# A mixer rebuilt: sums moved into the projections, branch b scaled between remainders, a norm's halves overlapped

## What is computed

```python
xn = rmsnorm(x)
h_a, c_a, b_a, v_b, g_b = split(xn @ w_in)                 # five groups of 512 channels
y_a = rmsnorm(b_a * dwconv(c_a * h_a, 3 taps))             # branch a
y_b = rmsnorm(silu(layernorm(dwconv(v_b * sigmoid(g_b), 31 taps) + bias)))   # branch b
h = x + concat(y_a, y_b) @ w_out
out = rmsnorm(h + peer(rmsnorm(h)))   # 8 heads, top 16 of 128 x 128 single-neuron experts each
```

## Time and profile before

| what | value |
|---|---|
| median of 3 runs | 1464.48 us (1464.34 to 1467.53) |
| profiled execution | 1464.40 us, span of its instructions 1462.6 us |
| PE busy | 1446.8 us, 99% |
| VectorE, ScalarE, POOL busy | 1232.1, 627.1, 880.1 us |
| mean granted clock of TensorE | 0.996 |

### The profile page before, as it was taken

The page is one execution under the profiler, slowest core; times in us unless marked ns, Lnnn a source line. Parts: engine busy times, 40 slices in busy tenths (PEclk is TensorE's granted clock), DMA queues, the critical chain, the costliest instruction groups (busy, mean ns, idle before and its releaser), DMA issues.

```text
span 1462.6 us, 25025 instructions
## 1 busy us (share of the span) xinstructions
PE 1446.8 (99%) x8592; PEld 1322.5 (90%) x8592; DVE 1232.1 (84%) x2517; ACT 627.1 (43%) x845; POOL 880.1 (60%) x551
## 2 busy tenths in 40 slices
PE   9998989999999999999999999999999999999998
PEld 9998989999999999999999999888888888888886
DVE  6998876899999999588788841799999999999995
ACT  6335543333333333566666654333333333333333
POOL 5687534556888888767666765255555555555510
PEclk9999999999999999999999999999999999999999
DMA  5321223567999999779999999899999999999962
GB/s 195 101 86 58 91 73 119 199 217 241 314 343 346 345 346 341 259 291 381 359 367 359 376 361 374 327 370 386 388 399 376 405 378 398 374 407 379 382 250 90
DMA packets 120260, 433.35 MB, mean 296 GB/s; under 512 B 12385, under 2 KB 12641, under 8 KB 118529
## 3 DMA queue, kind: packets, MB, share of 16 engines
q1 hardware_dynamic: 62592, 212.88, 40.5%
q0 software_dynamic: 46080, 167.79, 30.3%
q10 hardware_dynamic: 11520, 51.93, 8.9%
HBM read 379.34 MB, written 52.69 MB: 295 GB/s over the span
## 4 chain that ended last, share of the span: by engine, by line
PE 85%; DVE 0%; issue 0%; DVEq 0%; ACT 0%
PE ps_unit L861 37%; PE ps_misc L930 25%; PE ps_unit L930 12%; PE ps_unit L834 6%; PE ps_misc L896 3%; PE ps_misc L799 1%; PE ps_misc L803 0%; PE ps_unit L786 0%; PE ps_misc L926 0%; PE ps_unit L926 0%; PE ps_misc L915 0%; PE ps_misc L817 0%; DVE rows L1480 0%; DVE ps_unit L1478 0%; DVE hot_i L1649 0%
## 5 line engine op out<-in xcount | busy, mean ns | idle before, releaser
L515 POOL TENSOR_TENSOR w_lo<-raw,w_hi 128x1024 fp32r<-128x1024 f32 x171 | 412.1, 2412 | 200.6 <-issue 123.2
L579 POOL DMA_INDIRECT rows<-v_rows,expert x160 | 257.4, 1609 | 242.2 <-DVE sums L1490 162.7
L976 ACT ACTIVATE w_hi<-raw 128x1024 fp32r<-128x1024 f32 x300 | 315.2, 1051 | 43.7 <-ACT act_ring L1152 35.6
L1197 ACT ACTIVATE prod_hi<-prod 128x384 fp32r<-128x384 f32 x128 | 67.3, 526 | 335.0 <-PE ps_unit L930 334.3
L861 PE MATMUL ps_unit<-mov_hi,w_hi 128*128 128x384 f32 x1024 | 204.1, 341 | 0.0
L861 PE MATMUL ps_unit<-mov_hi,w_lo 128*128 128x384 f32 x1024 | 199.9, 337 | 0.0
L861 PE MATMUL ps_unit<-mov_lo,w_hi 128*128 128x384 f32 x1024 | 199.8, 337 | 0.0
L1480 DVE CUSTOM_DVE_ANT_0 rows<-rows,ps_unit 128x1024 f32<-128x1024 f32 x160 | 189.7, 1214 | 5.1 <-DMA rows<-u_rows,expert 5.0
L861 PEld LDWEIGHTS ps_unit<-mov_hi,w_lo 128*128 128x128 f32 x1024 | 180.9, 188 | 0.0
L861 PEld LDWEIGHTS ps_unit<-mov_lo,w_hi 128*128 128x128 f32 x1024 | 180.9, 188 | 0.0
L861 PEld LDWEIGHTS ps_unit<-mov_hi,w_hi 128*128 128x128 f32 x1024 | 177.5, 188 | 0.2 <-issue 0.2
(11 more groups left out here) (263 smaller groups left out, 2563.6 us busy)
## 6 DMA issues: line engine op xcount, KB each, us to landing
raw<-stream SPq DMA_DIRECT2D x300, 512.0 KB, 6.0
acts_dram<-act_ring ACTq DMA_DIRECT2D x64, 384.0 KB, 6.7
gates_dram<-gates ACTq DMA_DIRECT2D x12, 2048.0 KB, 9.9
acts_in<-acts_dram SPq DMA_DIRECT2D x32, 768.0 KB, 8.5
gates_even<-gates_dram SPq DMA_DIRECT2D x12, 1024.0 KB, 12.9
gates_odd<-gates_dram SPq DMA_DIRECT2D x12, 1024.0 KB, 12.7
rows<-u_rows,expert POOLq DMA_INDIRECT x160, 6.7
rows<-v_rows,expert POOLq DMA_INDIRECT x160, 8.4
```

The costliest lines, as they stand in the source:

```text
L515: nc.gpsimd.tensor_tensor(w_lo[:, j, :], raw[:, j, :], w_hi[:, j, :].bitcast(F32), ALU.subtract).then_inc(lo_made, 1)
L579: nc.gpsimd.indirect_dma_start(out=rows[:, n % ROWS_RING, :], out_offset=None, in_=table, in_offset=bass.IndirectOffsetOnAxis(ap=expert[:, ...
L976: nc.scalar.activation(w_hi[:, j, :], raw[:, j, :], ACT.Copy).then_inc(hi_made, 1)
L1197: nc.scalar.activation(prod_hi[:, v % RING], prod[:, v % 2], ACT.Copy).then_inc(prod_hi_made, 1)
```

## The change

It moves work and waits between engines; what is computed stays.

- The second sum of the first norm's squares is issued after three chunks of unit 1's last pass instead of six.
- VectorE scales projection 1 and makes the first padded chunk; POOL waits for it (`first_pad_made`). POOL makes the other three (`pad_b_made`).
- The sum of the convolution is issued inside projection 18, ahead of its fifth chunk, and that of the centred squares inside projection 19, ahead of its fourth. ScalarE squares ahead of its take of projection 18, and takes the root ahead of that of projection 19. The roots and the reciprocal get buffers of their own in `proj`.
- The last chunk of branch a: VectorE adds its taps (`taps_added`), POOL only multiplies by b.
- The first output unit is made chunk by chunk for both of its outputs, the high part of `mov` with both weights first, and the remainder `mov_lo` as it comes (`first_low`); the sum of a's squares stands between.
- VectorE's scalings of branch b (`scale_b`) stand between its `mov_low`s. The cache copies move behind the second `add_output`.
- The sum of b's squares moves behind the fourth output unit of branch a.
- The second norm: the sum of the first half is issued inside the last block of the last output unit; the second half's inside the first queries; VectorE's last output stands between the first norms; ten matmuls on ones (`keep_busy`) ahead of the queries; the two queries go side by side, in the second half three chunks apart.

```diff
@@ POOL
                     pool.wait_ge(rstd_made, 1)
+                    pool.wait_ge(first_pad_made, 1)
...
+                if u in (5, 7, 9):
+                    n = (u - 3) // 2
+                    pool.wait_ge(sigmoid_made, n + 1)
+                    pool.wait_ge(in_scaled, 2 * n)
...
+                    times(pad_b[:, n, 2 * HIST_B + T_PROMPT:PAD_B], proj[:, 2 * n, T_PROMPT:T],
+                          proj[:, 2 * n + 1, T_PROMPT:T]).then_inc(pad_b_made, 1)
...
+                    if c == WC - 1:
+                        step(times(b, b, rstd[:]))
+                        pool.wait_ge(taps_added, 1)
+                        times(h, h, b).then_inc(ya_made, 1)
+                        continue
@@ TensorE
+            def keep_busy(out, times):
+                for n in range(times):
+                    nc.tensor.matmul(out, ones[:], ones[:], start=True, stop=True)
...
-                    if k == KC - 2:
+                    if k == 3:
                         square_sum(sq[:, 0], sq_added, 1, True)
...
+            for j in range(RING):
+                pe.wait_ge(act_took, N_IN - RING + j - 1)
+                unit(N_IN // RING - 1, j, mov_hi, mov_lo, (None, None, sum_conv, sum_centred)[j], (0, 0, 4, 3)[j])
...
-            pe.wait_ge(conv_b_made, WC)
-            channel_sum(lambda c: proj[:, 2 * c], range(WC), WC, 0)
-            channel_sum(lambda c: sq[:, c], range(WC), WC, 1, SQ_X + WC - 1)
+            def first_low(k):
+                pe.wait_ge(mov_lo_made, KC + k + 1)
+                for o in range(2):
+                    ins = first_out(o, w_hi, mov_lo, k, last=(k == WC - 1))
...
+            for k in range(WC):
+                pe.wait_ge(mov_hi_made, KC + k + 1)
+                for o in range(2):
...
+                    first_out(o, w_hi, mov_hi, k, first=(k == 0))
+                    first_out(o, w_lo, mov_hi, k)
+                if k == WC - 2:
+                    first_low(0)
+                    first_low(1)
             pe.wait_ge(a_added, 1)
             pe.wait_ge(sq_made, SQ_X + 2 * WC)
             channel_sum(lambda n: sq[:, (WC, KC - 1)[n]], range(2), 2, 0)
-            pe.wait_ge(act_took, N_IN)
-            out_unit(0, 0)
+            first_low(2)
+            first_low(3)
             out_unit(0, 1)
             out_unit(0, 2)
+            out_unit(0, 3)
             pe.wait_ge(dve_took, WC)
             pe.wait_ge(silu_added, 1)
             channel_sum(lambda c: sq[:, c], (0,), 1, 1)
-            out_unit(0, 3)
...
+                        if a and o and k == 2:
+                            total(sq, 2, (sq_made, SQ_H + KC), 0, (0,))
...
-            total(sq, 2, (sq_made, SQ_H + KC), 0, (0,))
-            total(sq, 3, (sq_made, SQ_H + KC + 2), 0, (1,))
-            pe.wait_ge(dve_took, OUTPUTS)
+            pe.wait_ge(dve_took, OUTPUTS - 1)
...
+                for a, lag in ((0, 0), (1, 3)):
...
+                    for k in range(KC + lag):
+                        if a == 0 and k == 3:
+                            total(sq, 3, (sq_made, SQ_H + KC + 2), 0, (1,))
+                        for j, kj in ((0, k), (1, k - lag)):
...
+            keep_busy(ps_unit[:, 0, 0:P], BUSY_FFN)
             first_queries()
@@ ScalarE
+                if u == N_IN - 1:
+                    root(3, 1, 1.0 / WIDTH, out=std_c)
                 if u > 2 * WC and part == 2:
                     taps_of(c)
+                if u == N_IN - 2:
+                    for n in range(WC):
+                        act.wait_ge(centred, n + 1)
+                        nc.scalar.activation(sq[:, n], proj[:, 2 * n], ACT.Square).then_inc(sq_made, 1)
+                if u == N_IN - 1:
+                    act.wait_ge(unit_done, N_IN)
+                    group_high(0, proj[:, 2 * WC], par_col("out_a_g", 0))
                 if u > 0:
                     take(0, u, proj[:, u])
...
+                    if a == 0 and k == 1:
+                        last_square(KC - 1, 1)
+                    if a == 0 and k == 4:
+                        root_half(1)
@@ VectorE
+            reciprocal(2, rstd_c, std_c)
+            dve.wait_ge(taps_made, WC)
...
+            step(nc.vector.tensor_tensor(taps[0], taps[0], taps[1], ALU.add))
...
+            nc.vector.tensor_tensor(h[:, 0:T_PROMPT], taps[0][:, 0:T_PROMPT], taps[2][:, 0:T_PROMPT],
+                                    ALU.add).then_inc(taps_added, 1)
...
+            scale_b(0)
+            for c in range(2):
+                mov_low(KC + c, c, proj[:, 2 * WC + 3 * c], par_col("out_a_g", c))
+            scale_b(1)
+            for c in range(2, WC):
+                mov_low(KC + c, c, proj[:, 2 * WC + 3 * c], par_col("out_a_g", c))
+            scale_b(2)
+            scale_b(3)
...
+            last_output(0, 0)
+            last_output(0, 1)
+            last_add(0)
+            last_output(1, 0)
+            rstd_half(0)
+            norm(0, 0)
+            norm(1, 0)
+            norm_low(0, 0)
+            last_output(1, 1)
+            last_add(1)
             for a in range(2):
+                if a == 1:
+                    rstd_half(1)
+                    norm(0, 1)
+                    norm(1, 1)
+                for k in range(2, KC):
+                    norm(k, a)
+                    if a == 1 and k == 2:
+                        norm_low(0, 1)
+                    if k in (4, 6):
+                        norm_low(k - 2, a)
+                norm_low(KC - 2, a)
```

More of the change, by code:

```diff
@@ L99 @@
 MADE_AHEAD = AHEAD + 1
+BUSY_FFN = 10
 WARM_UP = 12
@@ L619, in _, with unit @@
         def _(pe):
-            def unit(lap, j, hi, lo):
+            def unit(lap, j, hi, lo, between=None, at=0):
                 u = RING * lap + j
@@ L626, in unit @@
                 for k in range(KC):
+                    if between and k == at:
+                        between()
                     for n, (w, m) in enumerate(((w_hi, hi), (w_hi, lo), (w_lo, hi))):
@@ L734, in out_unit, with first_out @@
                     last.then_inc(unit_done if o else out_half_done, 1)
-            pe.wait_ge(conv_b_made, WC)
-            channel_sum(lambda c: proj[:, 2 * c], range(WC), WC, 0)
-            channel_sum(lambda c: sq[:, c], range(WC), WC, 1, SQ_X + WC - 1)
+            def first_out(o, w, mov, k, first=False, last=False):
+                at = (WC * o + k) * P
+                for a in range(2):
+                    ins = nc.tensor.matmul(out_psum(o)[:, a, :], w[:, 0, at:at + P], half(mov[:, k], a),
+                                           start=first, stop=last)
+                return ins
+            def first_low(k):
+                pe.wait_ge(mov_lo_made, KC + k + 1)
+                for o in range(2):
+                    ins = first_out(o, w_hi, mov_lo, k, last=(k == WC - 1))
+                    if k == WC - 1:
+                        ins.then_inc(unit_done if o else out_half_done, 1)
+            pe.wait_ge(hi_made, FIRST_OUT + 1)
+            pe.wait_ge(lo_made, FIRST_OUT + 1)
+            for k in range(WC):
+                pe.wait_ge(mov_hi_made, KC + k + 1)
+                for o in range(2):
+                    if k == 0:
+                        pe.wait_ge(act_took, N_IN - 1 + o)
+                    first_out(o, w_hi, mov_hi, k, first=(k == 0))
[3 more added lines that the diff above has]
+                    first_low(1)
             pe.wait_ge(a_added, 1)
@@ L785, in first_queries @@
                             for m, (w, mov) in enumerate(((w_hi, mov_hi), (w_hi, mov_lo), (w_lo, mov_hi))):
[L786 to L790, removed]
+                                last = nc.tensor.matmul(unit_psum(j)[:, a, :], w[:, j, kj * P:(kj + 1) * P],
+                                                        half(mov[:, kj], a),
+                                                        start=(kj == 0 and m == 0), stop=(kj == KC - 1 and m == 2))
+                            if a == 1 and kj == KC - 1:
+                                last.then_inc(unit_done, 1)
             def head_scores(head, s):
@@ L1400, in add_output @@
                 nc.vector.tensor_tensor(halves(hid[:, k]), halves(hid[:, k]), out_psum(q), ALU.add).then_inc(dve_took, 1)
-            reciprocal(2, rstd[:])
-            dve.wait_ge(rstd_made, 2)
-            dve.wait_ge(centred, WC)
-            for c in range(WC):
-                nc.vector.tensor_tensor(proj[:, 2 * c], proj[:, 2 * c], rstd[:], ALU.mult).then_inc(scaled_b, 1)
-            reciprocal(3, rstd_a)
-            dve.wait_ge(rstd_made, 3)
-            for q in range(KC - 2):
+            reciprocal(3, rstd_a, std_a)
+            dve.wait_ge(rstd_made, 3)
+            for q in range(2):
+                add_output(q, rstd_a)
+            dve.wait_ge(pad_a_made, WC)
+            for pad, hist, at in ((pad_a, HIST_A, 0), (pad_b, HIST_B, CACHE_A)):
+                out = cache_out[:, at:at + WC * 2 * hist].rearrange("p (c s n) -> p c s n", c=WC, s=2)
+                nc.vector.tensor_copy(out[:, :, 0, :], pad[:, :, T_PROMPT:T_PROMPT + hist])
```

(3 more changed lines are left out.)

177 lines of the change are left out of this document (96 added, 81 removed).

## The result

| what | before | after |
|---|---|---|
| median (15 runs each) | 1464.8 us (1464.34 to 1467.53) | 1467.95 us (1466.69 to 1469.27) |
| profiled execution | 1464.40 us, span 1462.6 | 1466.69 us, span 1464.9 |
| ratio of after to before | | 1.0018, 95% interval 1.0011 to 1.0025 |

The change makes the kernel slower by 0.18%: a small loss that can be told from zero, and within the 0.3% that the prediction calls no change. The forecast was 1467.7 us. The profiled execution is the shortest of the 15 runs after, so its rows show 2.3 us of the loss of 3.15 between the medians; what is known of the rest comes with the experiments.

A forecast was written before the change was run, and what follows sets the result against it. The prediction took TensorE's work and the holes ahead of 214 us to bound the kernel. Its terms, 0.5 + 1.6 + 0.55 + 0.6 = +3.25 us on 1464.4, gave 1467.7 us, range 1459.5 to 1470.2.

The forecast's parts named there:

- The start and the convolution: First norm to fourth convolution: first reciprocal 0.88 us earlier, convolution starting at 27.45 instead of 31.73, ending at 121.4, not 129.54.
- Term 1: Branch a: POOL blocks VectorE's second remainder; second output unit starts at 151.6 against 151.12, +0.5 us, bounds -3.4 and +2.5.
- no blocking: Rival in branch a: VectorE's remainders come when their operands are there, unheld by POOL; 1461.2 us, chance 0.16.
- Term 2: TensorE's clock behind the waits in branch a: half of the shorter half-clock stretch, +1.6 us, bounds 0 and 2.8.
- Term 3: Branch b: VectorE's four remainders meet POOL again, its last output of branch a and the reciprocal 0.5 late; +0.55 us.
- Term 4: Second norm: first query earlier, second reciprocal 1.9 us late, shorter tail; +0.6 us, bounds -1.3 and +2.3.
- the clock holds: Rival: TensorE's clock stays up through both waits in branch a, adding 0 there; 1466.1 us, chance 0.15.
- slower: Rival: the clock falls in the second norm too, ahead of the second half's sum; 1469.4 us, chance 0.12 together with late sums.

The follow-up runs named there:

- sum_sooner: Changed kernel with the second half's sum of squares in the second norm ahead of chunk 2 of the first queries, not chunk 3: 1464.72 us, ratio to before 0.9995.
- pool_later: Changed kernel with POOL's weight subtraction for unit 21 held until VectorE has made all four remainders of branch a: 1464.28 us, ratio to before 0.9997.
- filled: Changed kernel with 5 and 9 matmuls on ones ahead of the first and second remainder on TensorE: 1465.31 us, ratio to before 0.9999.
- norm_as_before: Changed kernel with TensorE's, ScalarE's and VectorE's second-norm instructions put back to those of the kernel before: 1466.81 us, ratio to before 1.001.
- te_order: Changed kernel with TensorE taking all four remainders of the first output unit behind the sum of a's squares: 1466.8 us, ratio to before 1.0011.
- after_again: The changed kernel run once more, nothing edited: 1466.89 us, ratio to before 1.0015.
- the fastest version: Changed kernel, remainders behind a's squares' sum, unit 22's subtraction held, copies behind the sixth output, second norm's second sum one chunk sooner: 1461.3 us, ratio to before 0.9977.
- te_order_free: te_order plus POOL's weight subtraction for unit 22 held until VectorE has scaled all four chunks of b: 1465.77 us, ratio to before 1.0008.

## Why the prediction was right, step by step

**The start and the convolution.** Right to 0.4 us: reciprocal at 21.55 (21.43), convolution from 27.59 (27.45) to 121.76 (121.4), TensorE's wait for it 0.56 (0.4). The terms named for the start add up to 27.34 rather than 27.45.

**Term 1, branch a.** The mechanism was right: POOL's subtraction for unit 21 runs between the first and the second remainder, which ends at 146.8 (147.25). The size is told by `sum_sooner`, where the clock held: 4.51 us from 146.85 gives 151.36, +0.24 against +0.5. The two waits were smaller than worked out (1.22 and 2.03 for 2.2 and 2.5), since TensorE began the first three chunks half a microsecond later than worked out (139.47 for 138.95) and the second remainder came 0.45 sooner. `pool_later` decides between the prediction's forecast and its rival *no blocking*: taking away the meeting, and nothing else, gives the whole loss of the profiled execution back. The Trainium skill (SBUF — State Buffer, section "SBUF: two separate sides") has the shared pair of ports as an exclusive lock; the rows agree, since two remainders take 4.66 us beside the subtraction and 2.56 without it, and the second ends only behind POOL's instruction.

**Term 2, the clock.** +1.63 in the profiled execution against +1.6, and 1.56 by `filled`. That nearness is partly luck. By the method that gives 6.8 us for the longer stretch before, the shorter one is 3.4 and not 3.2 us, so its half is 1.7. And the fall is not one cost but differs from execution to execution, from 0 (`sum_sooner`) to 7.06 - 4.51 = 2.55 us (`norm_as_before`), almost the prediction's bounds of 0 and 2.8. The median of the 15 runs is 1.26 us above the profiled one. A fall as long as that of `norm_as_before` would add 0.92. That the longer runs lost more clock is on record (0.9969 against 0.9983), and that they lost it behind these two waits is likely by `filled`, where ten of eleven runs lie together at 0.999 to 1.000; how long their fall was is not shown, since none of them was profiled.

**Term 3, branch b.** Mis-sized: +0.32 against +0.55, inside its bounds. From the second output unit to b's second unit it takes 26.64 us (152.99 to 179.63), before 26.34; that is 0.30 of it. The four remainders of b did meet POOL (5.00 us together, 2.87 before), but the root was ready only at 174.27 and the reciprocal started at 174.41, so the meeting held it up by 0.1 and not by 0.5 us. TensorE also waits 1.13 us ahead of b's first unit, to 173.31, which the prediction doesn't have. The profile names no releaser; a VectorE output that the remainders had held up ended at 173.10. By the rows that wait cost nothing, since b's second unit starts only behind the first output after the reciprocal, which ended at 179.48.

**Term 4, the second norm.** Mis-sized: +0.12 against +0.6. The second reciprocal came 1.84 us later, as worked out (1.9), and TensorE waited for chunk 2 with the second half's sum behind it (1.24 instead of 1.8 us). What was mis-sized is the gain behind it: from the second reciprocal to the end of the queries it takes 10.46 us instead of 12.20, 1.74 less, where the prediction had 1.5 less and 0.2 more. `norm_as_before` shows the two sides of the exchange to be equal, and `sum_sooner` that the lateness was in the place of the sum alone: one chunk earlier gives 1.69 us back.

So the sum of the profiled execution is 0.24 + 1.63 + 0.32 + 0.12 = 2.3 against 3.25, and it is luck that the median lies within 0.3 us of the forecast. The sum starts from 1464.4, an execution of the kernel before from its lower group, and the median of the 15 runs after is one of the upper group; lower group against lower group (means of 1466.8 and some 1464.5) the change costs 2.3 us, and in the second set, median against median, 1.93. Of the rivals, *the clock holds* is what some executions do and not the median; *slower* fell, since the clock stayed at 1.00 from 198 to 219.

## What to carry to other kernels

When VectorE's instructions are taken off the critical path of one wait, look for the next POOL instruction that its order lets begin: the gain of `te_order` was lost twice in a row, to a weight subtraction that had come forward with it and to four small copies, and only with both out of the way did it reach the end. A POOL instruction with slack can be held by one wait until VectorE's urgent ones are through. Where a sum stands in TensorE's order behind a chunk that it doesn't need, it waits for that chunk, and moving it by one place was worth 1.69 us.

## What was not expected of the hardware

The clock behind the same two waits. Slices of 0.4 us from `norm_as_before`, where it fell in the second wait and stayed low:

```profile
145.20:145.60 0.40, 0.00 (x0) 0.00 (x0) 0.40 (x1) 0.00 (x0) 0.40 (x1) 0.95 0.00 0
145.60:146.00 0.40, 0.00 (x0) 0.00 (x0) 0.40 (x1) 0.00 (x0) 0.40 (x1) 0.50 0.00 0
...
152.00:152.40 0.40, 0.40 (x2) 0.34 (x1) 0.00 (x0) 0.00 (x0) 0.00 (x0) 0.52 0.00 0
```

and from `after_again`, where it fell at 146.5 and came back at 149.95:

```profile
146.40:146.80 0.40, 0.00 (x0) 0.00 (x0) 0.40 (x1) 0.00 (x0) 0.00 (x0) 0.67 0.00 0
...
149.60:150.00 0.40, 0.40 (x4) 0.40 (x3) 0.40 (x2) 0.00 (x0) 0.00 (x0) 0.56 0.00 0
```

With waits equal to 0.02 us in `norm_as_before`, `after_again`, after and `sum_sooner` the stretch at 1.2 GHz was 6.8, 3.4, 3.4 and 0 us long, as the slices at its two ends give it, and began at other moments. One profile therefore doesn't tell what such a hole costs; the times and mean clocks of all runs tell more. The spread was at most half a microsecond over ten of the eleven runs of `filled`, of `te_order` and of the fastest version, in which the two waits were filled, or replaced by one of 1.42 us.

The copies, with one operand from SBUF, waited for POOL's instructions as the two-operand ones did (1.47 us for one of 8 columns, from 156.79 to 158.26, beside the subtraction that ended at 158.23). The prediction had put them at nothing, and at half a microsecond without cover; in `te_order_free`, where the cover was gone, they took 2.9.
